# Where the one-column and gate sums stand, and products without a use in TensorE's waits: a transformer block on one core

## What is computed

```python
mod = silu(c) @ w_ada + b_ada                 # six vectors of 2048
h = rms_norm(x, g_pre_attn) * (1 + sc_a) + sh_a
proj = h @ w_in                               # q_a, k_a, v_a, q_b, ckv, k_pe
o_a = attention of 8 heads on 2 key heads     # RMS-normed q and k, rotary
o_b = latent attention of 8 heads             # keys and values from rms_norm(ckv) @ w_kv_b
o = concat(rms_norm(o_a, g_out_a), rms_norm(o_b, g_out_b)) @ w_out
x = x + gt_a * rms_norm(o, g_post_attn)
h = rms_norm(x, g_pre_mlp) * (1 + sc_m) + sh_m
y = square(relu(h @ w_mlp_in)) @ w_mlp_out    # 2048 -> 8192 -> 2048
x = x + gt_m * rms_norm(y, g_post_mlp)
```

## Time and profile before

| what | value |
|---|---|
| time, median of 3 runs | 2115.51 us (2113.52 to 2116.0) |
| the profiled execution, its own time | 2116.55 us |
| its span, first to last instruction | 2114.9 us |
| TensorE busy | 2061.8 us, 97% |
| VectorE / ScalarE / GpSimd busy | 1497.9 / 844.0 / 151.3 us |
| mean granted clock of TensorE | 0.991 |

### The profile page before, as it was taken

One profiled execution on the slowest core, in us unless ns is written; L12 is line 12 of the kernel. 1 busy time (PEld: TensorE's weight loads), 2 busy tenths in 40 slices (PEclk: granted clock), 3 DMA queues, 4 the chain that ended last, 5 costly groups with the idle time before them and its releaser, 6 DMA issues.

```text
span 2114.9 us, 26212 instructions
## 1 busy us (share of the span) xinstructions
PE 2061.8 (97%) x9314; PEld 1703.6 (81%) x9314; DVE 1497.9 (71%) x1804; ACT 844.0 (40%) x1153; POOL 151.3 (7%) x159
## 2 busy tenths in 40 slices
PE   6999999999999989999999999999999999999998
PEld 6787888887788878888888888888788888888886
DVE  5986898788877776445544554435789888888866
ACT  4454322587732363333222332233333333333422
POOL 0000000038600000000000000012000000000000
PEclk8999999999999999999999999999999999999999
DMA  8997868600277737655665566676657356456442
GB/s 296 341 307 221 274 202 251 197 22 11 91 258 251 245 123 249 206 189 200 223 222 186 182 218 228 201 237 224 246 225 265 135 214 258 151 206 238 179 179 80
DMA packets 214353, 435.20 MB, mean 206 GB/s; under 512 B 30180, under 2 KB 69768, under 8 KB 205448
## 3 DMA queue, kind: packets, MB, share of 16 engines
q1 hardware_dynamic: 196136, 361.43, 50.8%
q0 software_dynamic: 16704, 67.11, 8.9%
q10 hardware_dynamic: 1440, 5.70, 0.7%
HBM read 367.09 MB, written 67.11 MB: 205 GB/s over the span
## 4 chain that ended last, share of the span: by engine, by line
PE 83%; DVE 7%; DMA 3%; issue 3%; ACT 3%; POOL 1%; SPq 0%; DVEq 0%; ACTq 0%; POOLq 0%
PE bank L2085 11%; PE bank L2087 11%; PE bank L2086 11%; PE bank L2522 7%; PE bank L2523 7%; PE bank L2524 7%; PE bank L2072 6%; PE bank L2074 6%; PE bank L2073 6%; DMA raw<-in_w_ada 1%; PE bank L2573 1%; PE bank L2571 1%; PE bank L2572 1%; DMA w<-in_w_mlp_out 1%; PE bank L2143 1%
## 5 line engine op out<-in xcount | busy, mean ns | idle before, releaser
L1241 DVE TENSOR_TENSOR lo<-raw,hi 128x1024 fp32r<-128x1024 f32 (+2 forms) x234 | 275.6, 1182 | 377.2 <-ACT hi L728 375.2
L728 ACT ACTIVATE hi<-raw 128x1024 fp32r<-128x1024 f32 (+2 forms) x236 | 239.4, 1023 | 657.5 <-PE bank L2087 410.7
L2085 PE MATMUL bank<-h_hi,hi 128*128 128x512 f32 x1016 | 396.0, 390 | 0.0
L2087 PE MATMUL bank<-h_hi,lo 128*128 128x512 f32 x1016 | 395.3, 389 | 0.0
L2086 PE MATMUL bank<-h_lo,hi 128*128 128x512 f32 x1016 | 395.2, 389 | 0.0
L2522 PE MATMUL bank<-hi,y_use 128*128 128x512 f32 x784 | 307.6, 392 | 7.7 <-DVE acc L1968 3.8
L2523 PE MATMUL bank<-lo,y_use 128*128 128x512 f32 x784 | 306.2, 391 | 0.0
L2524 PE MATMUL bank<-hi,y_use 128*128 128x512 f32 x784 | 306.1, 390 | 0.0
L1184 ACT ACTIVATE hi<-w 128x1024 fp32r<-128x1024 f32 x168 | 178.3, 1062 | 296.8 <-PE bank L2524 218.3
L1892 DVE TENSOR_TENSOR lo<-w,hi 128x1024 fp32r<-128x1024 f32 x168 | 204.0, 1219 | 37.6 <-ACT hi L1184 37.1
L2085 PEld LDWEIGHTS bank<-h_hi,hi 128*128 128x128 f32 x1016 | 190.7, 188 | 40.1 <-issue 0.6
(11 more groups left out here) (319 smaller groups left out, 3114.2 us busy)
## 6 DMA issues: line engine op xcount, KB each, us to landing
raw<-in_w_ada SPq DMA_DIRECT2D x192, 512.0 KB, 5.0
raw<-in_w_mlp_in SPq DMA_DIRECT2D x128, 512.0 KB, 4.4
w<-in_w_mlp_out SPq DMA_DIRECT2D x128, 512.0 KB, 5.2
y_dram<-y_out POOLq DMA_DIRECT2D x32, 1792.0 KB, 8.8
y_use<-y_dram SPq DMA_DIRECT2D x53, 1024.0 KB, 8.9
raw<-in_w_in SPq DMA_DIRECT2D x32, 512.0 KB, 5.6
raw<-in_w_out SPq DMA_DIRECT2D x32, 512.0 KB, 5.0
raw<-in_w_in SPq DMA_DIRECT2D x48, 256.0 KB, 5.4
```

Source lines behind the costliest of these rows:

```text
L728: ins = nc.scalar.activation(dst, src, ACT.Copy)
L1241: ins = tt(dst, src, high.bitcast(F32), ALU.subtract)
L2085: mm(acc[n][:], wh, act_hi[:, k, :], start=first and q == 0, stop=False)
L2087: ins = mm(acc[n][:], wl, act_hi[:, k, :], start=False, stop=last and q == QROWS - 1)
```

## The change

Six places change; the numbers computed are the same.

- A helper `keep_busy` issues n products of 128x128 by 512 columns, whose results are not used: they go to a bank that nothing reads before it is written anew. It is called five times: 7 products ahead of the first `head_unit`, whose operand is the last row of `h_lo`, set to 1.0 by a memset on POOL; 4 ahead of the wait for the tile sums, 17 ahead of the fourth tile's transposes, and 4 behind these, between the sub-layers; and 11 between the two half groups of down group 0.
- The sums of squares are no longer issued together behind unit 1, but tile by tile behind each of the four tiles of unit 2.
- The four products of `spread_gm`, together ahead of unit 6, are now one each ahead of units 4, 5, 6 and 7 of that block; ScalarE's copies wait for all four.

```diff
-                        act.wait_ge(gm_reduced, 1)
+                        act.wait_ge(gm_reduced, NB)
...
+            def keep_busy(n, out_bank, held, moving):
+
+                for _ in range(n):
+                    mm(out_bank, held, moving, start=True, stop=True)
+
-            def unit_tokens(w, acc, act_hi, act_lo, k0, first, last, tiles=None, only=range(NT), behind_first=None):
+            def unit_tokens(w, acc, act_hi, act_lo, k0, first, last, tiles=None, only=range(NT), behind_first=None, behind=None):
...
+                    if behind and t < NT - 1:
+                        behind(t)
                 if t == NT - 1:
                     ins.then_inc(w_used, 1)
+                    if behind:
+                        behind(t)
...
             pe.wait_ge(x_t_ready, KD)
+            keep_busy(7, bank[0][:], h_lo[:, KD - 1, 0:P], h_lo[:, KD - 1, :])
             head_unit(0, 0)
...
-            def sum_squares():
-
-                pe.wait_ge(sq_ready, 2 * HEADS - 1)
-                pe.wait_ge(pt_done, 4 * 2 * HEADS)
-                pe.wait_ge(o_done, 2 * HEADS)
+            def sum_squares(t):
+
+                if t == 0:
+                    pe.wait_ge(sq_ready, 2 * HEADS - 1)
+                    pe.wait_ge(pt_done, 4 * 2 * HEADS)
+                    pe.wait_ge(o_done, 2 * HEADS)
                 for g in range(2):
-                    for t in range(NT):
...
+                if t == NT - 1:
+                    ins.then_inc(sq_reduced, 1)
...
-                    out_unit(n, j)
-                    if j == 1 and first:
-                        sum_squares()
+                    out_unit(n, j, behind=sum_squares if j == 2 and first else None)
...
+            keep_busy(4, bank[0][:], o_hi[:, KD - 1, 0:P], o_hi[:, KD - 1, :])
             pe.wait_ge(b_sum, 4 * NB)
             for t in range(NT):
+                if t == NT - 1:
+                    keep_busy(17, bank[0][:], o_hi[:, KD - 1, 0:P], o_hi[:, KD - 1, :])
                 pe.wait_ge(xn_ready, t + 1)
...
+            keep_busy(4, bank[0][:], o_hi[:, KD - 1, 0:P], o_hi[:, KD - 1, :])
             pe.wait_ge(row_done, 4 * NB)
...
-                if j == UNITS_D - 2:
-                    pe.wait_ge(y_done, (GROUPS - 1) * FCH)
-                    for n in range(NB):
-                        ins = mm(sets[1][n][:], ones[:], gm_acc[:, n * COLS:(n + 1) * COLS], start=True, stop=True)
-                    ins.then_inc(gm_reduced, 1)
+                if j >= UNITS_D - NB:
+                    n = j - (UNITS_D - NB)
+                    pe.wait_ge(y_done, (GROUPS - 1) * FCH - NB + n + 1)
+                    mm(sets[1][n][:], ones[:], gm_acc[:, n * COLS:(n + 1) * COLS], start=True, stop=True).then_inc(gm_reduced, 1)
...
             dn_products(0, 0)
+            keep_busy(11, bank[6][:], y_use[0][:, 0, 0, 0:P], y_use[0][:, 0, :, :].rearrange("p x n -> p (x n)"))
             pe.wait_ge(y_done, GROUPS * FCH)
...
+            nc.gpsimd.memset(h_lo[:, KD - 1, :].bitcast(F32), 1.0)
             nc.gpsimd.memset(ones[:], 1.0).then_inc(ones_ready, 1)
```

More of the change, by code:

```diff
@@ L2337, in wait_out, with out_unit @@
                     pe.wait_ge(r_ready, 1)
-            def out_unit(n, j, only=range(NT)):
-                unit_tokens(at_out(n, j)[1], sets[j // 4], o_hi, o_lo, QROWS * out_rows(j), j % 4 == 0, j % 4 == 3, only=only)
+            def out_unit(n, j, only=range(NT), behind=None):
+                unit_tokens(at_out(n, j)[1], sets[j // 4], o_hi, o_lo, QROWS * out_rows(j), j % 4 == 0, j % 4 == 3, only=only, behind=behind)
             def attend(H, nxt, values, values_n):
@@ L2398, in _ @@
             attend(2 * HEADS - 1, None, stage["v"], HEADS)
-            def sum_squares():
-                pe.wait_ge(sq_ready, 2 * HEADS - 1)
-                pe.wait_ge(pt_done, 4 * 2 * HEADS)
-                pe.wait_ge(o_done, 2 * HEADS)
-                for g in range(2):
-                    for t in range(NT):
[L2408 to L2413, removed]
+            def sum_squares(t):
[3 more added lines that the diff above has]
+                    pe.wait_ge(o_done, 2 * HEADS)
+                for g in range(2):
+                    c = 16 + 4 * g + t
+                    tile = slice(t * P, (t + 1) * P)
+                    ins = mm(bank[7][:, c:c + 1], sq_sum[:, g, tile], ones[:, 0:1], start=True, stop=g == 0)
+                    if g:
+                        ins = mm(bank[7][:, c:c + 1], sq[:, tile], ones[:, 0:1], start=False, stop=True)
+                if t == NT - 1:
+                    ins.then_inc(sq_reduced, 1)
             def spread_ga(n):
```

## The result

| | before | after |
|---|---|---|
| median of 11 runs, us | 2115.51 (2111.32 to 2119.39) | 2124.65 (2119.65 to 2130.19) |
| profiled execution: own time, span, us | 2116.55, 2114.9 | 2127.26, 2125.6 |
| mean granted clock of the span | 0.991 | 0.992 |

The changed kernel is slower. The ratio of after to before is 1.0049 [1.004, 1.0058], and the profiled pair differs by 10.7 us. The forecast was 2112.4 in a range of 2109.6 to 2115.2. Each ratio here is the one that its timing gives with its interval; it is not the plain quotient of two medians and can stand some 0.1% beside it.

The account below looks back on a forecast made before the run. TensorE, busy for 97% of the span, was taken to bound the kernel. At large, B -0.9, C -1.7, D -0.9 and A +0.5 gave -3.0 from 2115.5; forecast 2112.4 us, range 2109.6 to 2115.2.

Parts of the forecast that it names:

- The gate sums: Four products spread ahead of units 4 to 7, ScalarE's copies one unit later: 0 us, ends -0.1 and +0.3.
- the slower case: The prediction's slower outcome, rival 2: 2119.2 us, chance 0.06.
- B: Sums of squares, 583 to 586.6 us: spread over unit 2 they keep the clock up; -1.3 us, -0.9 at large.
- C: Ahead of the MLP, 761 to 767.5 us: 4, 17, 4 hidden fills, products behind at full pace; -1.7 us, -1.4 against profiled.
- rival 2: Ahead of the MLP the 17 fills meet a half clock, MLP starts 3.4 us late: 2119.2 us, chance 0.06.
- D: Between the first two down half groups, 1511.5 to 1518.4 us: 11 hidden fills; -0.9 us, -1.4 against profiled.
- A: Start, 30 to 44 us: 7 fills' gain does not last, longer wait at 57 us may drop the clock; +0.5 us.
- 3: Rival: all low stretches of C and D are the long kind, A costs nothing; -5.5 us, 2110.0, chance 0.25.
- rival 4: Groups of sums in B still bring the clock down: +0.25 instead of -1.3, 2114 us; chance 0.21 with Rival 1.
- Rival 1: Clock gains absorbed by VectorE or back as waits, C's -1.2 and A's +0.5 left: 2114.8; chance 0.21 with rival 4.

Follow-up runs that it names:

- f: Kernel before with only the fills between the sub-layers (4, 17, 4) added: 2112.48 us, ratio to before 0.9993.
- k: Kernel before with all the fills (7; 4, 17, 4; 11), gate sums and sums of squares as before: 2112.91 us, ratio 0.9994.
- l: Kernel before with all fills and the sums of squares spread over the tiles of unit 1, gate sums as before: 2111.33 us, ratio 0.9987.
- d: Kernel before with its four gate sums together one unit earlier, ScalarE's copies earlier too, no fills: 2113.87 us, ratio 1.0006.
- i: Kernel before with the sums of squares as one block, moved from behind unit 1 to behind unit 2: 2116.64 us, ratio 1.0014.
- e: Kernel before with only the 7 fills at the start and their memset added: 2112.21 us, ratio 0.9998.
- h: Kernel before with only the sums of squares spread over the tiles of unit 2: 2118.94 us, ratio 1.0017.
- j: Kernel before with only the sums of squares spread over the tiles of unit 1, last sum ready when it was before: 2113.0 us, ratio 0.9996.
- g: Kernel before with only the 11 fills between the down half groups added: 2113.24 us, ratio 1.0000.
- b: Kernel before with only the gate sums spread, one each ahead of units 4 to 7: 2122.73 us, ratio 1.0043.
- c_gate_spread_early: Changed kernel with the four gate sums one each ahead of units 2 to 5, ScalarE's copies one place earlier: 2115.19 us, ratio to before 1.0009.
- a: Changed kernel with its gate sums put back together ahead of unit 6, all else kept: 2115.73 us, ratio to before 1.0012.

## Why the prediction was wrong

**The gate sums: the step that failed.** The prediction wrote: "ScalarE's copies start one unit later and must be done within the last unit of the block: 2.1 us in 5.4. I take 0, with ends -0.1 and +0.3 (four changes of kind)." TensorE's own cost was as said, 0.2 us, and the copies were in time for TensorE. But `gm_copied` has a second reader, POOL, and behind POOL stand `comb_m_ready`, SyncE and the saves of `y`. Measured alone: +0.43%, 9 us. So the failed step is a term put at 0 after a look at one reader of the semaphore only. No rival held it; the slower case was another mechanism and had 0.06. The row that would have told it was POOL's first add in before, 1419.50 against copies that ended at 1419.09: 0.4 us of slack where the edit moved the copies by 5.4.

**B.** The size was right: three more changes of kind, the clock full, 1.6 us gained between 580 and 591 where 1.3 was forecast; the cover of unit 4 held, as no wait stands there. What failed is "about 1.7 us of cover left" as the only cover looked at. The low parts of units 4 and 5 also free the raw buffers of later units, which this left out; the wait on `comb` gives the 1.6 us back, and alone the edit costs 0.17% instead of gaining. "POOL's loads behind the same semaphore are for a much later stage" was wrong too: two of them bring the rows for `comb`, some 30 us on. And the clock fell behind the block of sums in all seven traces that have it behind unit 1, not in two of three. With the last sum on time the cost is gone (0.9996).

**C.** Right. The fill was hidden, the clock stayed at 1.00, the gain in the trace was 1.4 us, as forecast against this execution (1.4 too in `f`, `k` and `l`), and 0.9993 is the size, if not clear of 1. The table of `f_between_fill_alone` shows a granted clock of 1.00 over the fills, the transposes and the products behind them, so rival 2 is out. By the rule of the Trainium skill that was weighed there ("TensorE: Matmul & The Clock Gate", Part 4) the transposes could have let it fall; these traces, with 1.00 over them, do not bear that out.

**D.** In after the place is no longer the one that was costed: the wait grew from 2.87 us to 2.50 of fill and 3.89 of wait, and the clock fell all the same. In `k_fills_only` and `l`, where fill and wait (2.50 and 0.85) are near the old 2.87, what the step foretold is there: the clock is kept, and waits on `lo` of 0.85 and 1.1 us take the place of the one of 2.87 (forecast: one of 1.2). Worth alone, 1.0000: the -0.9 was too much, by an amount that lies within the interval of 0.1%. One reason can be seen: before's profiled execution was the costliest of its kind. Of the six traces of other kernels with neither this fill nor late gate sums, `d`, `f` and `i` keep the clock at D with waits of 1.65 to 1.87 us, and `e`, `h` and `j` lose it for 3.4 us where before lost it for 6.8.

**A.** The first half was right: 1.5 us sooner at 43.5, nothing left at 57. The price was of the right kind, a wait of 2.03 us (2.2 forecast) ahead of the one-column sums and a clock that falls at them, but it was 3.2 us in after's trace, where +0.5, at most +1.4, was said: the clock stayed down for 6.8 us, and 13 products were slow where I had counted 7, the one-column sums ahead of them too. Over many executions it is small, 0.9998 alone. Traces of kernels without this fill have the clock fall at 57 us too (`g`, `h`, `i` and `j`, not before, `b`, `d` or `f`), so part of this price is paid without the fill. Why it falls in one execution and not in another stays open. One thing lies outside of that step. In before the half clock covers transposes and one-column sums ahead of the wait as well: 16 such sums took 3.41 us at 31.83. In `b`, whose clock stayed full until 35.3, they took 1.84 us, the first product of the query heads came at 37.23 instead of 40.00, and 2.8 us of lead were left behind 57. The fill stands behind that place and can't win it.

**Rivals.** 3 and 4 are out by the trace of after (A cost 3.2 us, and the clock at B was 1.00), 2 by the clock over C. Rival 1, gains absorbed by VectorE, describes A and D, though the fills with timely sums still gave 0.13%.

**The arithmetic.** Some figures of the prediction do not follow from their own terms: 2115.5 - 3.0 is 2112.5, not 2112.4; the range ends 0.4 us outside of rivals 1 and 3 (2114.8 and 2110.0); and rival 4 gives -1.85, not -1.5. None of this bears on the miss.

## What to carry to other kernels

When a product is moved or spread, list every reader of the semaphore that its last piece raises, and follow each through its engine's whole queue (here ScalarE, POOL, SyncE, VectorE) to the next wait of the engine that bounds; the slack is that of the tightest reader, not of the nearest. Spread sums backwards, over the work ahead of the old place, so that the last one keeps its time. Fill waits and break up one-column groups only where the semaphores keep their times: then it was worth 0.13% here, and one unit of lateness in the wrong place cost three times as much.

## What the runs showed of the hardware

- Half clock stood behind, or set in during, waits of TensorE of about 2 us, ahead of one-column sums or of a late operand: 2.03 us at 57.02 in after, 1.87 us at 619.56 in `h`, 2.31 us at 734.34 in `i`, 2.35 us at 1511.63 in `g`. In `l` waits of 0.84, 1.1 and even 1.84 us (at 731.45) were not followed by it, nor was one of 1.87 us at 1509.29 in `f`. At the one-column sums near 57 us half clock followed waits of 1.1 to 1.2 us in `g`, `h`, `i` and `j`, and did not follow one of 1.33 us in before.
- One low stretch lasted from 3.4 us (`h` at 620.86) to 13.7 us (before, `f` and `h`, from 30 us on). One of 10.2 us lies in `c_gate_spread_early` from 735.4, behind a wait of 2.25 us. It has 16 one-column records inside, so that these sums, too, ran at half pace (3.41 us where before took 1.84):

```profile
734.17 0.50 PE L2456 MATMUL bank<-hi,o_hi 128*128 128x512 f32 x1 [2.25 <-DVE lo L1241]
...
737.59 3.41 PE L2467 MATMUL bank<-ones,mod_acc 128*128 128x1 f32 x16
```

- At C the traces of kernels without the fills have a low stretch of 6.8 us (before, `g`, `j`) or 10.2 us (`b`, `d`, `e`, `h`, `i`), and those with them have none (`f`, `k`, `l`, `a`, `c`, after). Before's execution happened to hold the short kind.
